# Index scores of the sample sequences as quarter-array products, and an earlier split of the gated attention, in a hybrid decoder trunk

## What is computed

```python
def dsa_attend(q, qi, wi, k, v, ki, q_pos, top_k):
    dots = jnp.einsum('bthd,bsd->bths', qi.astype(F32), ki.astype(F32)) * (IDX_DIM ** -0.5)
    score = jnp.einsum('bths,bth->bts', jax.nn.relu(dots), wi.astype(F32))
    ...
    _, idx = lax.top_k(score, top_k)
```

```python
    y_att = (attn * jax.nn.silu(zga)) @ w_attn_out
    ...
    out = (g_att * y_att + g_conv * y_conv) @ w_out
```

## Time and profile before

| | us |
|---|---|
| median of 3 runs | 3641.19 |
| lowest and highest of them | 3640.60, 3641.64 |
| profiled execution, its own time | 3645.13 |
| its span, first to last instruction | 3643.4 |
| TensorE busy (share of the span) | 3512.0 (96%) |
| VectorE, ScalarE, GpSimd busy | 1775.0, 1070.1, 1168.0 |
| mean granted clock of TensorE (1 = 2.4 GHz) | 0.982 |

### The profile page before, as it was taken

How to read it: one execution, slowest core, us unless ns; L and a number is a source line. 1 busy time by engine, 2 the same in 40 slices (tenths; PEclk the granted TensorE clock), 3 DMA queues, 4 the chain that set the end, 5 groups by cost and what they waited for, 6 DMA issues and landing times. The chain is left out here.

```text
span 3643.4 us, 66828 instructions
## 1 busy us (share of the span) xinstructions
PE 3512.0 (96%) x27774; PEld 3250.0 (89%) x27774; DVE 1775.0 (49%) x2514; ACT 1070.1 (29%) x1504; POOL 1168.0 (32%) x476
## 2 busy tenths in 40 slices
PE   6899999998999999999999999999989999999999
PEld 3699988988989888998888999898889998899999
DVE  1413578968969113232115145788688771233201
ACT  2222222223452333221223222222235423332221
POOL 0233323423324222333232333234233232224433
PEclk9799999999999999999999999999999999999999
DMA  9733334655534764558895555443322247644332
GB/s 319 252 102 102 97 101 109 182 163 158 179 122 130 242 220 164 197 192 274 288 287 169 163 159 167 126 127 104 103 88 89 83 154 239 209 142 137 124 124 96
DMA packets 557131, 590.49 MB, mean 162 GB/s; under 512 B 73564, under 2 KB 523377, under 8 KB 546747
## 3 DMA queue, kind: packets, MB, share of 16 engines
q1 hardware_dynamic: 556828, 586.21, 51.2%
HBM read 546.37 MB, written 116.39 MB: 182 GB/s over the span
## 5 line engine op out<-in xcount | busy, mean ns | idle before, releaser
L785 POOL TENSOR_TENSOR w_lo_t<-raw,w_hi_t 128x1024 fp32r<-128x1024 f32 x472 | 1167.8, 2474 | 2458.6 <-ACT w_hi_t L794 2458.6
L1081 PE MATMUL acc<-act_hi,w_hi_t 128*128 128x272 f32 x6528 | 1411.5, 298 | 54.8 <-DVE u_s L1585 14.3
L1081 PE MATMUL acc<-act_hi,w_lo_t 128*128 128x272 f32 x6528 | 1358.8, 290 | 0.0
L1081 PE MATMUL acc<-act_lo,w_hi_t 128*128 128x272 f32 x6528 | 1356.5, 289 | 0.0
L1081 PEld LDWEIGHTS acc<-act_hi,w_hi_t 128*128 128x128 f32 x6528 | 1037.2, 190 | 141.5 <-issue 106.9
L1081 PEld LDWEIGHTS acc<-act_lo,w_hi_t 128*128 128x128 f32 x6528 | 1035.6, 190 | 0.0
L1081 PEld LDWEIGHTS acc<-act_hi,w_lo_t 128*128 128x128 f32 x6528 | 1029.4, 191 | 0.0
L794 ACT ACTIVATE w_hi_t<-raw 128x1024 fp32r<-128x1024 f32 x472 | 499.8, 1059 | 1678.3 <-PE acc L1081 1652.4
L1623 DVE SCALAR_TENSOR_TENSOR conv<-conv,cw 128x512 f32<-128x512 f32 x240 | 199.7, 832 | 65.6 <-POOL w_lo_t L785 65.6
L1081 PE MATMUL acc<-m_hi,w_hi_t 128*128 128x272 f32 x1024 | 215.8, 292 | 0.0
L1081 PE MATMUL acc<-m_hi,w_lo_t 128*128 128x272 f32 x1024 | 211.5, 288 | 0.0
(11 more groups left out here) (240 smaller groups left out, 2704.8 us busy)
## 6 DMA issues: line engine op xcount, KB each, us to landing
raw<-in_w_in_dram SPq DMA_DIRECT2D x272, 512.0 KB, 3.5
ada_ring<-in_w_ada_dram SPq DMA_DIRECT2D x95, 512.0 KB, 7.0
raw<-in_w_in_dram SPq DMA_DIRECT2D x136, 256.0 KB, 3.2
k_near<-in_cache_k_dram SPq DMA_DIRECT2D x256, 128.0 KB, 2.6
v_near<-in_cache_v_dram SPq DMA_DIRECT2D x256, 128.0 KB, 2.6
k_ring<-k_near SPq DMA_DIRECT2D x64, 512.0 KB, 5.2
v_page<-v_near SPq DMA_DIRECT2D x64, 512.0 KB, 6.1
raw<-in_w_out_dram SPq DMA_DIRECT2D x64, 512.0 KB, 4.3
```

The costliest lines, as they stand in the source:

```text
L785: pool.tensor_tensor(w_lo_t[:, m % 2], raw[:, m % 4], w_hi_t[:, m % 2].bitcast(F32), ALU.subtract).then_inc(S.w_lo, 1)
L1081: last = pe.matmul(acc[:, 2 * m + h, 0:HALF], w[:, c % 2, k, P * m:P * m + P], r[:, kt, h * HALF:(h + 1) * HALF], start=first and k == 0 a ...
```

## The change

It has two parts.

1. `qi_blk` has 64 columns for each sequence, without zeros. `dots_s` becomes one step (s = 1) of four matmuls of 64 rows, 64 columns and 512 tokens, each on another quarter of the array: row half p and column half c = (f + p) mod 2, into bank p. One relu of 1,024 columns follows, and one mixing step (s = 3) of four matmuls with 64 rows and 32 columns, which read the row half where the products lie. s = 2 holds nothing. `turn_kx` waits for the relu instead of the key copy, since both now use banks 0 and 1. The semaphore counts go from 17 to 9 a layer.
2. The split of the prompt columns of attention tiles 8 to 11 moves from chunk 0 of group 43 to chunk 3 of group 42, ahead of the combination's copies; that of tiles 12 to 15 moves ahead of ScalarE's wait for chunk 0. The sample columns of all eight tiles are split in one more pair of instructions. The chunks 2 and 3 of group 43 wait for all 17 splits.

```diff
-        qi_blk = at(C + 9408, "qi_blk", [P, SEQS, P])
+        qi_blk = at(C + 9408, "qi_blk", [P, SEQS, 64])
...
-                    elif s <= 2:
-                        f = 17 * l + 2 * b + s
-                        act.wait_ge(S.sdots_ready, f)
-                        if 2 * b + s > 2:
-                            act.wait_ge(S.mixed, f - 2)
-                        act.activation(relu_s[:, s - 1, :], aux[:, 2, :], ACT.Relu).then_inc(S.srelu_done, 1)
+                    elif s == 1:
+                        act.wait_ge(S.sdots_ready, 9 * l + b + 1)
+                        if b >= 1:
+                            act.wait_ge(S.mixed, 9 * l + b)
+                        act.activation(relu_s[:, :, :], aux[:, 0:2, :], ACT.Relu).then_inc(S.srelu_done, 1)
...
-                    act.wait_ge(S.ag_done, l + 1)
+                    act.wait_ge(S.gp_done, 8 * l + k - 7)
                     act.wait_ge(S.w_used, w_chunk(l, N_MG - 1, k // 4) + 1)
-                    act.activation(act_hi[:, k, :], q_att[:, k - 8, :], ACT.Copy).then_inc(S.split_hi, 1)
+                    act.activation(act_hi[:, k, 0:SEQ], q_att[:, k - 8, 0:SEQ], ACT.Copy).then_inc(S.split_hi, 1)
+
+            def split_samples(l):
+
+                act.wait_ge(S.ag_done, l + 1)
+                act.wait_ge(S.w_used, w_chunk(l, N_MG - 1, 3) + 1)
+                act.activation(act_hi[:, 8:16, SEQ:TOK], q_att[:, :, SEQ:TOK], ACT.Copy).then_inc(S.split_hi, 1)
...
-                if n == N_MG and i == 0 and half == 1:
-                    for k in range(8, 16):
+                if n == N_MG - 1 and i == 3 and half == 0:
+                    for k in range(8, 12):
                         split(l, k)
+                if n == N_MG and i == 0 and half == 0:
+                    for k in range(12, 16):
+                        split(l, k)
+                    split_samples(l)
...
-                        pe.wait_ge(S.split_lo, 16 * l + 4 * i + 4)
+
+                        pe.wait_ge(S.split_lo, 17 * l + (4 * i + 4 if i < 2 else 17))
...
-                need(pe, S.kx_copied, 8 * l + b)
+                need(pe, S.srelu_done, 9 * l + b)
...
-            def dots_s(l, b, f):
+            def dots_s(l, b):
+
                 pe.wait_ge(S.kx_copied, 8 * l + b + 1)
                 pe.wait_ge(S.diag_done, l + 1)
-                need(pe, S.srelu_done, 17 * l + 2 * b + f)
-                if b == 0 and f == 0:
-                    pe.wait_ge(S.conv_s_done, 8 * l + 8)
-                pe.matmul(aux[:, 2, :], qi_blk[:, b, :], kx_t[:, f, :], start=True, stop=True).then_inc(S.sdots_ready, 1)
+                for f in range(2):
+                    for p in range(2):
+                        c = (f + p) % 2
+                        last = pe.matmul(aux[64 * c:64 * c + 64, p, :], qi_blk[64 * p:64 * p + 64, b, :], kx_t[64 * p:64 * p + 64, f, :],
+                                         start=True, stop=True)
+                last.then_inc(S.sdots_ready, 1)
...
-                for p in range(2):
-                    j = 2 * f + p
-                    last = pe.matmul(aux[32 * j:32 * j + 32, 3, :], mixw[:, p, b, :], relu_s[:, f, :], start=b == 0, stop=b == SEQS - 1)
+                for f in range(2):
+                    for p in range(2):
+                        c, j = (f + p) % 2, 2 * f + p
+                        last = pe.matmul(aux[32 * j:32 * j + 32, 3, :], mixw[64 * c:64 * c + 64, c, b, :], relu_s[64 * c:64 * c + 64, p, :],
+                                         start=b == 0, stop=b == SEQS - 1)
                 last.then_inc(S.mixed, 1)
...
-                    if 1 <= s <= 2:
-                        dots_s(l, b, s - 1)
-                    if s >= 2:
-                        mix_s(l, b, s - 2)
+                    if s == 1:
+                        dots_s(l, b)
+                    if s == 3:
+                        mix_s(l, b)
...
-                st.then(dve.memset(qi_blk[:, :, :], 0.0))
-                st.wait()
...
-                dve.tensor_tensor(q_att[:, t, 0:SEQ], q_att[:, t, 0:SEQ], gate[:, t % 4, 0:SEQ], ALU.mult)
+                dve.tensor_tensor(q_att[:, t, 0:SEQ], q_att[:, t, 0:SEQ], gate[:, t % 4, 0:SEQ], ALU.mult).then_inc(S.gp_done, 1)
...
+                if n == N_MG - 1 and i == 3 and half == 1:
+                    for k in range(8, 12):
+                        rest_of(l, k)
                 if N_GLU <= n < N_MG:
                     window(l, 8 * (n - N_GLU) + 2 * i + half)
...
-                    for k in range(8, 16):
+                    for k in range(12, 16):
                         rest_of(l, k)
+                    rest_of_samples(l)
```

More of the change, by code:

```diff
@@ L532, in load_ada @@
                 if d == ADA_FIRST:
-                    sp.wait_ge(S.split_lo, 16)
+                    sp.wait_ge(S.split_lo, 17)
                 if ada_slot(d) == 7:
@@ L1195, in turn_kx, with mix_s @@
                 last.then_inc(S.kx_turned, 1)
-            def dots_s(l, b, f):
+            def dots_s(l, b):
                 pe.wait_ge(S.kx_copied, 8 * l + b + 1)
                 pe.wait_ge(S.diag_done, l + 1)
-                need(pe, S.srelu_done, 17 * l + 2 * b + f)
-                if b == 0 and f == 0:
-                    pe.wait_ge(S.conv_s_done, 8 * l + 8)
-                pe.matmul(aux[:, 2, :], qi_blk[:, b, :], kx_t[:, f, :], start=True, stop=True).then_inc(S.sdots_ready, 1)
-            def mix_s(l, b, f):
-                pe.wait_ge(S.srelu_done, 17 * l + 2 * b + f + 1)
-                if b == 0 and f == 0:
+                for f in range(2):
[4 more added lines that the diff above has]
+                last.then_inc(S.sdots_ready, 1)
+            def mix_s(l, b):
+                pe.wait_ge(S.srelu_done, 9 * l + b + 1)
+                if b == 0:
                     pe.wait_ge(S.u_copied, 8 * l + 8)
                     pe.wait_ge(S.state_taken, 8 * l + 8)
-                for p in range(2):
-                    j = 2 * f + p
-                    last = pe.matmul(aux[32 * j:32 * j + 32, 3, :], mixw[:, p, b, :], relu_s[:, f, :], start=b == 0, stop=b == SEQS - 1)
+                for f in range(2):
[3 more added lines that the diff above has]
+                                         start=b == 0, stop=b == SEQS - 1)
                 last.then_inc(S.mixed, 1)
             def dots_tail(l):
-                pe.wait_ge(S.srelu_done, 17 * l + 16)
+                pe.wait_ge(S.srelu_done, 9 * l + 8)
+                pe.wait_ge(S.conv_s_done, 8 * l + 8)
                 for b in range(SEQS):
-                    last = pe.matmul(aux[0:64, 2, STEPS * b:STEPS * b + STEPS], qi_blk[0:64, b, 0:64],
+                    last = pe.matmul(aux[0:64, 2, STEPS * b:STEPS * b + STEPS], qi_blk[0:64, b, :],
                                      ki_new[0:64, SEQ + STEPS * b:SEQ + STEPS * b + STEPS], start=True, stop=True)
@@ L1222, in mix_tail @@
             def mix_tail(l):
-                pe.wait_ge(S.srelu_done, 17 * l + 17)
+                pe.wait_ge(S.srelu_done, 9 * l + 9)
                 for b in range(SEQS):
@@ L1635, in turn_qi @@
                         src = qi[64 * h:64 * h + 64, :, SEQ:TOK].rearrange("p j (b t) -> p b j t", t=STEPS)
-                        c0 = 64 * p + 32 * h
-                        last = dve.tensor_copy(qi_blk[64 * p:64 * p + 64, :, c0:c0 + 32].rearrange("p b (j t) -> p b j t", t=STEPS), src)
+                        last = dve.tensor_copy(qi_blk[64 * p:64 * p + 64, :, 32 * h:32 * h + 32].rearrange("p b (j t) -> p b j t", t=STEPS), src)
                 last.then_inc(S.diag_done, 1)
@@ L1824, in window @@
                 if h == H_KTAIL + 2:
[L1825 removed]
+                    dve.wait_ge(S.mixed, 9 * l + 9)
                     st.then(dve.tensor_copy(sc4[:, :], aux[:, 3, :]))
@@ L1877, in gated_attn, with rest_of_samples @@
                     dve.wait_ge(S.ao_p, 16 * l + 16)
-                dve.tensor_tensor(q_att[:, t, 0:SEQ], q_att[:, t, 0:SEQ], gate[:, t % 4, 0:SEQ], ALU.mult)
+                dve.tensor_tensor(q_att[:, t, 0:SEQ], q_att[:, t, 0:SEQ], gate[:, t % 4, 0:SEQ], ALU.mult).then_inc(S.gp_done, 1)
                 dve.tensor_copy(ga_s[:, t, :], gate[:, t % 4, SEQ:TOK]).then_inc(S.ga_used, 1)
             def rest_of(l, k):
-                dve.wait_ge(S.split_hi, 16 * l + k + 1)
-                src = yc[:, k, :] if k < 8 else q_att[:, k - 8, :]
-                dve.tensor_tensor(act_lo[:, k, :], src, act_hi[:, k, :].bitcast(F32), ALU.subtract).then_inc(S.split_lo, 1)
+                dve.wait_ge(S.split_hi, 17 * l + k + 1)
+                src, n = (yc[:, k, :], TOK) if k < 8 else (q_att[:, k - 8, 0:SEQ], SEQ)
+                dve.tensor_tensor(act_lo[:, k, 0:n], src, act_hi[:, k, 0:n].bitcast(F32), ALU.subtract).then_inc(S.split_lo, 1)
+            def rest_of_samples(l):
+                dve.wait_ge(S.split_hi, 17 * l + 17)
+                dve.tensor_tensor(act_lo[:, 8:16, SEQ:TOK], q_att[:, :, SEQ:TOK], act_hi[:, 8:16, SEQ:TOK].bitcast(F32),
```

(1 more changed line is left out.)

6 lines of the change are left out of this document (3 added, 3 removed).

## The result

| | time, us | profiled execution | its span | granted clock |
|---|---|---|---|---|
| before, 4 runs | 3641.39 median (3640.6 to 3641.64) | 3645.13 | 3643.4 | 0.982 |
| after, 4 runs | 3599.61 median (3598.55 to 3604.22) | 3598.8 | 3597.0 | 0.983 |

The ratio is 0.9888 [0.9871, 0.9905]: 41.8 us less by the medians, where 41.0 were forecast. The two profiled executions are 46.3 us apart. By the start times of the main matmuls, 4.6 of these lie outside the stages that the change touches, most of it in the first twelve weight groups of layer 0 (326.78 against 323.16 us) with no edit near. There the profiled execution of before waits 3.35 us for `w_lo` at 150.92; no other trace here has that wait in layer 0. So these 4.6 us are put down to the two executions and not to the change.

A forecast was written before the change was run, and what follows sets the result against it. TensorE, busy for 96% of the span, was taken to bound the kernel. Index products 24.5 us plus merge 16.5 gave 41.0, so 3641.19 - 41.0 = 3600.2 us; its own range 3595 to 3606, the whole range 3595 to 3615.

The forecast's parts named there:

- Product piece 1.22, mixing piece 1.17, 1.70 a sequence: TensorE's index products: pieces beside the main matmuls take 1.22 and 1.17 us, 2.39 a sequence against 4.09, 1.70 less.
- The step beyond the trace: Index products: tiles split by rows and columns at once run together; the trace showed only each split by itself.
- the first rival: Index products: tiles sharing a bank or row half run in turn, 0.87 us more 16 times, 3614.1 us; chance 0.09.
- the slower one: Index products: quarters run one after another, 3.48 + 0.3 us a piece, 39.0 us slower, 3680.2 us; chance 0.04.
- The bank rule: Mixing piece: a documented ban on different row tiles accessing one PSUM bank simultaneously; the forecast took nothing for it.
- `w_lo` comes at a time that VectorE sets: First index sequences: VectorE's unbroken work holds `w_lo` until 707.9, so TensorE waits away 1.35 us gained a layer.
- Later VectorE is free, 4.9 us of 15.3: Later index sequences: VectorE works 10.45 of 17.00 us, so 1.70 less leaves 4.9 us spare.
- No later `w_lo` wait: Index scores: TensorE waits about 1.8 us for `w_lo` at sequence 1's first chunk, and never later.
- The merge gives 8.25 a layer: Merge: moving splits earlier removes TensorE's 5.60 us wait and 2.49 of slow clock, 8.25 us a layer, 16.5 in all.
- The rival of a remaining wait: Merge: VectorE or GpSimd still ends late, 2 to 16.5 us come back, 3608 us for a middle case; chance 0.09.
- The sum: Whole kernel: 24.5 us from the index products plus 16.5 from the merge, 41.0 us less; forecast chance 0.78.
- Index part, 24.5 forecast: Index products: 8 x 1.70 less 1.35 us is 12.25 a layer, 24.5 in two layers.

The follow-up runs named there:

- e5: Changed kernel with the second pair of index products sent through the first pair's quarters, so they take turns and half the scores are lost; 3609.35 us, one run.
- e6: Changed kernel with all four mixing matmuls reading row half 0, so half of what is mixed is wrong; 3595.05 us, one run.
- e8: Changed kernel with 44 of VectorE's convolution taps a layer left out beside the first sequences, so the convolution is wrong; 3595.99 us, one run.
- e3: Changed kernel with about 9 of VectorE's convolution taps moved to later windows and none left out; 3595.68 us.
- e4: The changed kernel itself, run again unaltered as the reference on its chip; 3599.03 us.
- e10: Changed kernel with ScalarE's copies for tiles 12 to 15 and the samples left behind its wait for chunk 0, four splits still in group 42; 3602.57 us.
- e9: Changed kernel with all eight prompt splits in group 43, ahead of ScalarE's wait for chunk 0, none in group 42; 3600.37 us.
- e1: Kernel with the changed index products and the merge of the kernel before; 3612.49 us, ratio 0.9925 to the kernel before.
- e2: Kernel with the changed merge and the index products of the kernel before; 3621.63 us, ratio 0.9946 to the kernel before.

## Why the prediction was right, point by point

- *Product piece 1.22, mixing piece 1.17, 1.70 a sequence.* Right: 1.22 and 1.19; 2.41 from 4.09 is 1.68. The step beyond the trace, rows and columns split at once, held, and e5 shows what it would have cost otherwise: 0.84 for the 0.87 of the first rival. That rival falls, and with it the slower one, the quarters one after another.
- *The bank rule.* Right to take nothing. The Trainium skill (TensorEngine Tiling (Array Packing), Restrictions and Gotchas) says that different row tiles cannot use one PSUM bank at the same time. After does so in each mixing piece, on different partitions, and e6, where no two row halves write it, takes the same 1.06 and 0.99 us. In this form, with each row half on its own partitions, the measurement speaks against reading the rule as a cost.
- *`w_lo` comes at a time that VectorE sets.* The mechanism is right, shown by e8 and e3 from VectorE's side and by e5 from TensorE's. Place and price are less so. I forecast 1.76 us at the first chunk of sequence 1; the waits are 1.90 to 2.14 us, six at that place and eight one chunk later. I also had it that 1.76 us a layer would come back if GpSimd got in at another moment. That is wrong: in those eight layers it did get in, and the stream held the next subtraction instead, at the same price. The mis-sized term is the clock behind the wait: 2.49 us are in my sum for the merge's wait and nothing for this one. Behind 7 of the 14 waits the rows are 0.45 apart for some 3.6 us, which costs 1.5 us (eight rows from 702.37 to 706.00 take 3.63 instead of the 2.1 that they and the change of shape need). After had it in layer 0 and not in layer 1, and that is about half of the 2.5 us between its index gains of 9.8 and 12.3 where 12.25 were forecast: the stretch (19,2) to (20,3) differs by 1.3. The other 1.3 lie in (24,0) to (25,3), where the clock is longer down behind the wait for the convolution's sum in layer 0, though that wait is 4.2 us in both. In e4, which had the slow clock behind neither `w_lo` wait, the gains are 12.4 and 12.7.
- *Later VectorE is free, 4.9 us of 15.3.* Wrong in size, at no cost. Window of two later sequences of after (columns as in the earlier trace rows):

```profile
740.00:755.30 15.30, 15.30 (x123) 13.36 (x122) 12.94 (x18) 4.73 (x5) 6.83 (x2) 1.00 0.64 173
755.30:770.60 15.30, 15.30 (x123) 13.36 (x122) 13.01 (x17) 4.62 (x5) 6.56 (x2) 1.00 0.73 210
```

  VectorE has about as many instructions as in the earlier trace rows, 17 or 18, but is busy for 13.0 us, since in each of these sequences one instruction is drawn out beside GpSimd's subtraction (2.50 us for 0.55 at 742.45, 2.88 for 0.75 at 757.57). 2.3 us are spare, less than half of what I counted on. I took the busy time of one old window and carried it over into a shorter period. That window held no such clash: its two subtractions took 2.39 us each. The windows of 17 us from 703 and 720 in before have 14.69 and 14.71 us busy.
- *No later `w_lo` wait.* Wrong: one of 0.92 us came at 824.17 in after, behind the last sequence, and one as long in layer 1. In e4 it isn't there. It is small, and the next wait, that for the convolution's sum, is shorter where it stands (4.2 us against 5.0 in e4).
- *The merge gives 8.25 a layer.* Right as far as it was worked out. The stretches (43,0) to (44,0) are shorter by 9.2 and 9.2: 2.5 of it behind the old wait, as said, and 6.7 before, the wait's 5.76 and about 1.0 of slow clock after the combination. Whether that 1.0 is the change's own can't be told, as this stretch differs from layer to layer and from execution to execution: (43,0) to (43,2) takes 12.1 to 14.9 us in the nine kernels without the wait. The rival of a remaining wait falls for after, and e10 shows how near it was: 1.11 us with five splits late. I gave the move into group 42 its share of the credit; e9 shows that it has none.
- *The sum.* 41.0 against 41.8 looks better than its terms are. Index part, 24.5 forecast: 22.1 in the profiled pair, 25.1 in e4, 26.7 by the medians of e1. Merge, 16.5 forecast: 19.6 in the profiled pair, 17.6 by the medians of e2. In the profiled pair the two errors have opposite signs, by the medians the same one, and there the two parts add up to 3 us more than forecast where both together gave 40.2. So each part is known to 1 to 3 us, and that the sum came out within 0.8 is in part luck.

## What to carry to other kernels

A matmul whose stationary block holds zeros can be cut into quarters of the array, and four quarters in different rows and columns take one round, plus a change of tile shape (an estimate: 1.22 and 1.19 less the 0.87 of a full product, about 0.3 us). When TensorE gets shorter it catches up with engines that it used to trail, so ask of each producer what sets its time. Where that is another engine's unbroken stream, thin the stream just ahead of the deadline; that the producer gets in once doesn't help if the stream goes on. Read how busy an engine is from several windows, not from one. Before work is moved far ahead, see whether it is enough to put it in front of its engine's next wait, as the merge's splits show.

## What the runs showed of the hardware

- **VectorE's taps and GpSimd's subtraction hold each other up, and who gets in isn't fixed.** The Trainium skill (SBUF — State Buffer, Who interferes with whom) says that the port pair they share is locked exclusively, and that issue order decides who blocks. The rows agree with the lock. GpSimd's subtraction takes 2.4 us alone. When it gets in, VectorE's instruction of 0.75 takes 2.88. When it doesn't, it stands as long as VectorE issues one instruction behind another: 8.0 us at this place in before, 9.1 to 9.7 in after, 3.3 to 5.6 in later sequences of after. Issue order, as far as the start times show it, doesn't tell who gets in. VectorE's rows ahead of the clash in layer 0, in after and then in e4, which is the same kernel:

```profile
692.07 0.74 DVE L1639 SCALAR_TENSOR_TENSOR conv<-conv,cw 128x512 f32<-128x512 f32 x1
692.73 0.75 DVE L1639 SCALAR_TENSOR_TENSOR d_odd<-conv,cw,d_odd 128x512 f32<-128x512 f32 x1
```

```profile
693.20 0.74 DVE L1639 SCALAR_TENSOR_TENSOR conv<-conv,cw 128x512 f32<-128x512 f32 x1
693.86 2.89 DVE L1639 SCALAR_TENSOR_TENSOR d_odd<-conv,cw,d_odd 128x512 f32<-128x512 f32 x1
```

  GpSimd starts at 692.60 in one and 693.73 in the other, 0.13 us ahead of VectorE's second row both times, and the outcome is the opposite. The two layers of after differ in the same way, and of the 14 layers it got in in eight. What decides it stays open.
- **The same wait of 1.9 to 2.1 us sometimes lowers TensorE's clock and sometimes not,** 7 of 14 times, also within one execution: three of the six waits at chunk (20,1) and four of the eight at (20,2). Behind the 0.91 to 0.95 us of `w_lo` waits at chunk (24,1) it stayed up all 14 times that the traces here have, behind 1.11 us in both layers of e10 too, and behind 5.60 it was at the lower level of 1.2 GHz in both layers of before and of e1. A removed wait of 1.9 to 2.1 us is worth its own length or 1.5 us more.
